# State-space loop: the backward direction's triangle rows made by ScalarE, the forward ones by GpSimd

## The reference

```python
acs = jnp.cumsum(a.reshape(b, nc, Q, G, hg), axis=2)          # Q = 128 tokens a chunk, 2 chunks
lower = jnp.tril(jnp.ones((Q, Q), dtype=bool))[:, :, None, None]
seg = acs[:, :, :, None] - acs[:, :, None, :]
decay = jnp.exp(jnp.where(lower, seg, -jnp.inf))
cb = jnp.einsum('bcign,bcjgn->bcijg', Cm, Bm)
y = jnp.einsum('bcijgh,bcjghp->bcighp', cb[..., None] * decay, xdt)
...
h_T, h_in = lax.scan(step, h0, (states, chunk_decay))
y = y + jnp.einsum('bcign,bcghpn->bcighp', Cm, h_in) * jnp.exp(acs)[..., None]
```

## Time and profile before

| | |
|---|---|
| median of 3 runs | 1223.58 us (1223.34 to 1224.31) |
| the profiled execution | 1223.86 us, its span 1221.8 us, mean granted clock of TensorE 0.992 |
| busy, TensorE | 1172.3 us (96% of the span) |
| busy, VectorE | 712.3 us (58%) |
| busy, ScalarE | 490.9 us (40%) |
| busy, GpSimd | 27.3 us (2%), 31 instructions |
| the chain that ended last | TensorE 85%, VectorE 10%, ScalarE 2% |
| the state-space stage | from about 848 to 905 us of the span |

### The profile page before, as it was taken

How to read it: one execution, slowest core, us unless ns; L and a number is a source line. 1 busy time by engine, 2 the same in 40 slices (tenths; PEclk the granted TensorE clock), 3 DMA queues, 4 the chain that set the end, 5 groups by cost and what they waited for, 6 DMA issues and landing times.

```text
span 1221.8 us, 18381 instructions
## 1 busy us (share of the span) xinstructions
PE 1172.3 (96%) x7498; PEld 953.6 (78%) x7498; DVE 712.3 (58%) x1185; ACT 490.9 (40%) x740; POOL 27.3 (2%) x31
## 2 busy tenths in 40 slices
PE   4999989999999999999999999999889999999998
PEld 3777765677688888888887668898446798999998
DVE  3499988843542333323333378977979645556544
ACT  4343225652443332222222433455148736554442
POOL 0100000000000000000000000001500000000000
PEclk9999999999999999999999999999999999999999
DMA  9645336016553222333124553434224157546632
GB/s 359 251 149 196 130 135 219 1 61 216 172 172 104 86 68 88 133 108 104 64 62 150 197 187 115 127 107 154 77 45 139 36 173 256 193 133 216 202 112 96
DMA packets 124333, 170.72 MB, mean 140 GB/s; under 512 B 4797, under 2 KB 112743, under 8 KB 120039
## 3 DMA queue, kind: packets, MB, share of 16 engines
q1 hardware_dynamic: 121430, 164.99, 40.5%
q10 hardware_dynamic: 2833, 4.74, 1.5%
HBM read 168.63 MB, written 1.08 MB: 139 GB/s over the span
## 4 chain that ended last, share of the span: by engine, by line
PE 85%; DVE 10%; ACT 2%; issue 2%; DMA 1%; ACTq 0%; SPq 0%; DVEq 0%; POOL 0%
PE acc L1923 22%; PE acc L1925 22%; PE acc L1924 22%; PE pmod L1862 2%; PE acc L1985 1%; PE p L1810 1%; PE acc L1987 1%; PE acc L1986 1%; PE acc L2516 1%; PE p L2542 1%; DVE seg L1714 1%; PE acc L1810 1%; DVE Y L1267 1%; DMA xin<-in_ctx 1%; PE p L2145 1%
## 5 line engine op out<-in xcount | busy, mean ns | idle before, releaser
L555 DVE TENSOR_TENSOR w_lo<-raw,w_hi 128x1024 fp32r<-128x1024 f32 x234 | 259.0, 1148 | 245.6 <-ACT w_hi L545 245.4
L545 ACT ACTIVATE w_hi<-raw 128x1024 fp32r<-128x1024 f32 (+1 forms) x236 | 221.6, 987 | 435.4 <-PE acc L1925 400.2
L1923 PE MATMUL acc<-Hhi,w_hi 128*128 128x512 f32 (+1 forms) x976 | 334.9, 343 | 6.9 <-POOL ptap L624 4.5
L1924 PE MATMUL acc<-Hlo,w_hi 128*128 128x512 f32 (+1 forms) x976 | 332.3, 340 | 0.0
L1925 PE MATMUL acc<-Hhi,w_lo 128*128 128x512 f32 (+1 forms) x976 | 332.2, 340 | 0.0
L1923 PEld LDWEIGHTS acc<-Hhi,w_hi 128*128 128x128 f32 x976 | 186.6, 191 | 32.1 <-issue 9.0
L1925 PEld LDWEIGHTS acc<-Hhi,w_lo 128*128 128x128 f32 x976 | 186.5, 191 | 20.3
L1924 PEld LDWEIGHTS acc<-Hlo,w_hi 128*128 128x128 f32 x976 | 186.6, 191 | 20.1
L1923 PE MATMUL acc<-hid_hi,w_hi 128*128 128x512 f32 (+1 forms) x448 | 157.1, 351 | 0.0
L1924 PE MATMUL acc<-hid_lo,w_hi 128*128 128x512 f32 (+1 forms) x448 | 155.7, 348 | 0.0
L1925 PE MATMUL acc<-hid_hi,w_lo 128*128 128x512 f32 (+1 forms) x448 | 155.7, 348 | 0.0
(11 more groups left out here) (328 smaller groups left out, 1390.9 us busy)
## 6 DMA issues: line engine op xcount, KB each, us to landing
raw<-in_mod_w SPq DMA_DIRECT2D x48, 1024.0 KB, 5.3
raw<-in_ffn_w_in SPq DMA_DIRECT2D x44, 1024.0 KB, 5.1
raw<-in_od_w_in SPq DMA_DIRECT2D x15, 1024.0 KB, 5.3
raw<-in_ffn_w_out SPq DMA_DIRECT2D x16, 768.0 KB, 4.2
raw<-in_ev_w_in SPq DMA_DIRECT2D x10, 1024.0 KB, 7.7
raw<-in_ffn_w_out SPq DMA_DIRECT2D x16, 640.0 KB, 3.9
raw<-in_od_w_out SPq DMA_DIRECT2D x8, 1024.0 KB, 5.2
raw<-in_ev_w_out SPq DMA_DIRECT2D x8, 768.0 KB, 6.1
```

What stands on the lines that cost most here:

```text
L545: nc.scalar.activation(w_hi[:, w % 2, c0:c1], raw[:, r % RAW_SLOTS, c0:c1], ACT.Copy)\
L555: nc.vector.tensor_tensor(w_lo[:, w % 2, c0:c1], raw[:, r % RAW_SLOTS, c0:c1], w_hi[:, w % 2, c0:c1].bitcast(F32), ALU.subtract).then_inc( ...
L1923: mm(outs[m], hi[:, j, cols], xh, start=(first and j == 0), stop=False)
L1924: mm(outs[m], hi[:, j, cols], xl, start=False, stop=False)
```

## The change

GpSimd makes the forward `rx` tiles alone, one instruction a segment in place of two, and raises `rx_forward`. ScalarE makes the backward ones, in four Copies a segment, one for each head, with the column of `dts` as the activation's scale; the last raises `rx_backward`. Segments 0 and 1 are made between its other instructions ahead of the loop, segment 2 right before the DMA issues `rows_out` 2 to 5, and segment k + 2 inside round k, after Exp(k), for k = 1 to 5. TensorE waits for one counter or the other. What is computed stays the same.

```diff
@@ gpsimd @@
                 if k >= 2:
                     pool.wait_ge(s("seg_mm"), k - 1)
-                for d in range(2):
-                    at_ = 32 * c + 16 * d + 4 * b
-                    nc.gpsimd.tensor_tensor(rx[:, (2 * k + d) % 4, :].rearrange("p (h i) -> p h i", h=4),
-                                            cst(("upto", "from")[d]).unsqueeze(1).to_broadcast([P, 4, P]),
-                                            dts[:, 7, at_:at_ + 4].unsqueeze(2).to_broadcast([P, 4, P]), ALU.mult)\
-                        .then_inc(s("rx_ready"), 1)
+                at_ = 32 * c + 4 * b
+                nc.gpsimd.tensor_tensor(rx[:, 2 * k % 4, :].rearrange("p (h i) -> p h i", h=4),
+                                        cst("upto").unsqueeze(1).to_broadcast([P, 4, P]),
+                                        dts[:, 7, at_:at_ + 4].unsqueeze(2).to_broadcast([P, 4, P]), ALU.mult)\
+                    .then_inc(s("rx_forward"), 1)
@@ scalar @@
+            def backward_rows(k):
+
+                b, c = SEG[k]
+                if k >= 2:
+                    act.wait_ge(s("seg_mm"), k - 1)
+                for h in range(4):
+                    col = 32 * c + 16 + 4 * b + h
+                    ins = A(rx[:, (2 * k + 1) % 4, h * P:(h + 1) * P], cst("from"), ACT.Copy, scale=dts[:, 7, col:col + 1])
+                ins.then_inc(s("rx_backward"), 1)
+
             act.wait_ge(s("row_stored"), 32)
             act.wait_ge(s("cb_mm"), 1)
             rows_out(0)
             rows_out(1)
+            act.wait_ge(s("da_ready"), 1)
+            backward_rows(0)
             for k in range(4):
                 act.wait_ge(s("xw_used"), (2, 2, 5, 5)[k])
                 A(state[:, k // 2 * 2, k % 2, :], stbank[k // 2 * 4 + k % 2], ACT.Copy).then_inc(s("state_act"), 1)
+                if k == 1:
+                    backward_rows(1)
             act.wait_ge(s("xw_used"), 6)
...
+            backward_rows(2)
             for q in range(2, 6):
                 rows_out(q)
             for k in range(8):
...
                 A(seg[:, (2 * k + 1) % 4, :], RB[k % 3][:, :], ACT.Exp).then_inc(s("decay_ready"), 1)
+                if k and k + 2 < 8:
+                    backward_rows(k + 2)
                 if 1 <= k < 6:
                     act.wait_ge(s("inter_mm"), k)
@@ tensor @@
                 for d in range(2):
-                    pe.wait_ge(s("rx_ready"), 2 * k + d + 1)
+                    pe.wait_ge(s("rx_backward" if d else "rx_forward"), k + 1)
```

## The result

The changed kernel takes 1225.72 us in the median of 22 runs (1224.56 to 1226.39), the kernel before 1223.72 (1223.04 to 1225.18) beside it. The ratio is 1.0015, with a 95% interval of 1.0009 to 1.0021: 2.0 us slower, clear of noise, but inside the 0.2% that the prediction called the same. Forecast were 1224.7 and a range of 1221.5 to 1227.2. The profiled execution took 1225.9 us, its span 1224.1 against 1221.8.

What follows compares the result with a forecast made beforehand. VectorE was taken to bound the stage to about 885 us, then a ring of TensorE and ScalarE. The 3.4 us saved go back through late start and ring, leaving 1223.58 + 1.1 = 1224.7 us, range 1221.5 to 1227.2.

Steps and rivals of the forecast that it cites:

- Steps (1) and (3): GpSimd loses eight tiles, saving VectorE 3.4 us, 0.45 of it ahead of the loop; ScalarE's Copy rounds 0 and 1 free.
- Step (2): On ScalarE, one 128x128 Copy with a column as scale takes 0.40 us, four overlapping ones 1.3 us.
- Step (4): Ahead of the loop, segment 2's Copies make the first Exp 1.5 us late; saved collisions pay all but 0.2 us.
- Step (5): In the loop TensorE and ScalarE wait on each other through the Copies: turns 4.9 or 5.5 us, stage end +1.1 us.
- Rival C: TensorE's clock dips inside the loop in the new gaps, twice the size at 910 to 915: 1226.9 us; chance 0.05.
- Rival A: In rounds 2 to 5 VectorE sets the pace and four Copies take 0.5 us: 1221.0 us; chance 0.10.
- Rival B: Four Copies take 2.0 us, or DMA issues ahead of the loop wait behind them: 1227 to 1228.5 us; chance 0.16.
- Rival D: VectorE's long multiplies have another cause than GpSimd, and ScalarE has room: nothing moves, 1223.6 us; chance 0.04.

Runs made afterwards that it cites:

- relief_only: Changed kernel without ScalarE's Copies for segments 2 to 7 and TensorE's waits for them, so those backward rows are not made; 1220.0 us, 0.9971 of before.
- only_ahead: Changed kernel with ScalarE making backward rows of segments 0 and 1 only, GpSimd all the others; 1222.77 us, 0.9994 of before.
- after_table: Changed kernel plus a tiny Exp behind the state copies, so Exp's table loads in ScalarE's idle time; 1222.28 us, 0.9989 of before.
- early_rows: Changed kernel with the backward Copies one round earlier in ScalarE's loop, before its wait for inter_mm; 1222.9 us, 0.9992 of before.
- one_copy: Changed kernel with one 128x512 Copy per segment in place of four 128x128, all heads using the first head's column; 1224.62 us, 1.0003 of before.
- forward_twice: Changed kernel with GpSimd making every forward tile twice, sixteen tiles as in the kernel before; 1225.23 us, 1.0016 of before.
- before_again: The kernel before, unchanged, run and profiled once more; 1223.59 us.
- before_table: Kernel before plus a tiny Exp behind the state copies, so Exp's table loads in ScalarE's idle time; 1223.62 us, 1.0001 of before.
- fill_gaps: Changed kernel with TensorE making the forward product of decays(4), (5) and (6) twice, to work while it waits; 1225.8 us, 1.0016 of before.
- after_again: The changed kernel, with nothing altered, run and profiled once more; 1226.04 us, 1.0020 of before.
- early_table: Changed kernel with backward Copies one round earlier and a tiny Exp behind the state copies loading Exp's table early; 1220.49 us, 0.9973 of before.

## Why the prediction was right

- Steps (1) and (3), the relief: 3.2 us measured (relief_only) for 3.4, and 0.45 ahead of the loop for 0.45 (only_ahead). VectorE did set the pace until 885 in the kernel before.
- Step (2), four Copies: 1.26 to 1.28 us for 1.3, one of them 392 ns in the mean for 400. The line between the 2- and 256-column rows held. By the figures of the Trainium skill, "ScalarE: Activation LUTs", What ACT_TABLE_LOAD costs, one Copy is 386 ns and four are 1.27 us, an estimate; the trace agrees.
- Step (4), the late start: the first Exp 1.43 us late from the root for 1.5, and Exp(2) +0.26 for +0.2. The DMA issues did run beside the Copies. What I had not taken apart: the late start itself was worth 1.7 us (after_table), cancelled to 0.3 by collisions saved.
- Step (5), the ring: turns of 4.92, 5.50, 4.90 and 5.66 for 4.9, 5.5, 4.9 and 5.7, Exp(6) +1.15 from the root for +1.1. early_rows takes the ring away and its 2.9 us come back; one_copy shrinks it by the length of the Copies; forward_twice shows that VectorE has slack under it.
- The sum said +1.1, measured were +2.0. What it lacks is no instruction's time but TensorE's clock: in the profiles 0.9 us behind the ring and 0.6 in the attention. Step (5) had put both at nothing ("the rest is equal"), and that sentence failed. Rival C had named a dip with a chance of 0.05 and the wrong place and reason; its price of 2.2 us is near the 1.8 that the two dips of after cost by the marks. Dips of this kind come in nearly every profile, before included; what was missing in the sum is a term for them. By the marks they cost, from the root to the first output projection, 0 us in two profiles, 0.4 to 1.1 in the three of before, before_again and before_table, 1.8 in both of after and 2.6 in fill_gaps. The range held because it was wide enough for a term that was not in it.
- Rival A fell with the Copies at 392 ns: one_copy, at 0.71 us in place of the 1.0 from which A was to decide, still was not faster. Its total has a dip in it; by its Exp(6) less the 1.64 of the dip, 44.5 against 45.0, it would have been ahead by 0.5 us, an estimate. So A's break-even was not far off: only its Copies do not exist. Rival B fell with the issues that ran beside the Copies. Rival D fell with relief_only.

How much of the 0.9 us beyond the forecast belongs to the change? The mean clocks of all runs speak for most of it, and they point at the late start and not at the ring. At 0.991 or lower are 28 of the 32 runs of after and after_again, and 26 of the 95 of the kernel before. after_table, with the same ring and an early first Exp, has 1 of 11; early_rows, without the ring but with the late first Exp, 9 of 11, and fill_gaps, with both, 10 of 11. What these late kernels share in the trace is TensorE's wait ahead of intra(0). It is 1.81 or 1.82 us in all five profiles with a first Exp at 18.0, and under 0.8 us in every other (forward_twice, whose first Exp is later still, has 0.67, 0.71 and 0.70 us in place of the one wait, and 2 of 11 runs at 0.991 or lower):

```profile
868.77 0.66 PE L2485 MATMUL acc<-seg,HF 128*64 128x128 f32 x8 [0.38 <-DVE seg L1714]
```

This one is of before. In three of the five a dip at 870 follows, and in no other profile. If that is the cause, step (4) priced the late start by the waits of the instructions alone (+0.2) and left out what it does to TensorE's clock. It is not shown: profiles and clocks go together here, but no run changes that one wait and nothing else.

Not settled: why both profiles of after have their dip at 902 and not at 870, why a dip falls at 901 in one of two of before, and nowhere in after_table and forward_twice. What can be said is that 1.15 us of the loss are the ring and the late start, and that the dips' part is no wait of any instruction.

## What to carry to other kernels

Work moved off an overloaded engine must not land between a wait and its answer on the engine that takes it: ask of each moved instruction which wait it stands behind and who waits for what stands behind it, and issue it one round ahead where the buffers allow. Where such a move delays a function that needs a new table, load the table with a tiny activation in idle time; it paid where the first Exp was what the others waited for (after_table, early_table) and not where VectorE was busy until then (before_table). And before pricing a slow multiply on VectorE, look at whether GpSimd was reading at the time.

## What the runs showed of the hardware

- TensorE's half-speed stretches, about 3.4 us each at 0.50, come and go between executions of the same program (before and before_again) and between programs that differ by one tiny activation (before and before_table). The same wait of TensorE does not always bring one: 1.65 us ahead of intra(7) stand in all 13 profiles, with a dip starting 0.8 to 1.7 us behind the wait's end in seven of them and none there in six.
- One dip costs 0.7 to 1.6 us of the stage and 0.2 to 0.9 of the attention, by what TensorE has to do in it. That is more than most terms of this change, so differences below 0.1% need the marks inside the profile and the mean clock of each run, and not the total alone.
- VectorE's collisions with GpSimd hit single instructions: a 128x32 `qsc` scaling (L1695) took 0.89 us beside a GpSimd tile in the kernel before, and 0.18 without one after the change.
